# Hybrid decoder block: the gate's low-rank product in plain f32 over four column groups, x rejoined by GpSimd

## The chip, the cores and the metric

The kernel runs on one core of a Trainium2 chip. The metric is the device time of one execution in microseconds. Three runs of the kernel before gave 302.15, 302.29 and 302.38; the median is 302.29. One further execution was profiled, and the rows below come from it.

## The reference

One decoder block on 256 tokens of width 1024, all in float32. The part that matters here is the gate of the gated linear attention (GLA): its logits go through a product of rank 16.

```python
h = rms_norm(x, norm1_gain[l])
proj = h @ w_in[l]
gq, gk, gv, gr, g_low, mq, mk, mv = parts          # g_low is 16 columns of proj
gate_logit = (g_low @ w_gate_up[l] + b_gate[l]).astype(jnp.float32)
log_a = jax.nn.log_sigmoid(gate_logit) / GLA_GATE_TAU
o_gla = gla_chunked(gq, gk, gv, log_a)             # then norm, times silu(gr)
q_m, k_m = rotary(mq, positions), rotary(mk, positions)
o_moba = moba_attention(q_m, k_m, mv)              # causal softmax attention here, then norm
x = x + jnp.concatenate([o_gla, o_moba], axis=-1) @ w_out[l]
h = rms_norm(x, norm2_gain[l])
x = x + (silu(h @ w_ffn_gate[l]) * (h @ w_ffn_up[l])) @ w_ffn_down[l]
return rms_norm(x, final_norm_gain)
```

## The kernel before

**Products in halves.** Each large product splits both operands into a rounded half (hi, type fp32r) and the rest (lo) and takes three matmuls: hi·hi, hi·lo, lo·hi. Weights arrive in `raw` (three slots, 512 columns by 4 chunks, or the like, of 2048 elements a unit). ScalarE (ACT) casts a unit to `w_hi` (L877), VectorE (DVE) subtracts to get `w_lo` (L1137), and counts `lo_ready`; both rings have six slots. Units are numbered: 0 to 11 are six blocks of 512 columns of w_in (q and k of the GLA, q, k, v of the attention, v and r of the GLA), 12 to 15 w_out, then three to a phase of the feed-forward part. TensorE (PE) takes them in order and waits for `hi_ready` and `lo_ready` at the head of each (`unit_ready`).

**The start.** Tokens are transposed on TensorE into PSUM (`aux`), in eight chunks of 128 features. ACT scales each by the norm's gain into `aT_hi` (L900) and DVE makes `aT_lo` (L1141), so that the chunk x is held as two halves. Units 0 and 1 are worked on chunk by chunk: `first_row(k)` takes six matmuls for chunk k (L562, L565, L568), with the weights' halves made just ahead by ACT (L906) and DVE (L1158). DVE's queue alternates: L1141 of a chunk, L1158 of the same chunk. The semaphores are `xT_lo_ready` and `first_lo_ready`.

**The gate's product.** After the eight chunks `gate_low` computes g_low transposed, 16 values by 256 tokens. Its weights, `low_raw` (128 x 8 chunks x 16), are split by ACT (L916) and GpSimd (POOL, L477) into `low_w`, where a chunk's 128 columns hold the hi and lo halves of the 16 columns in turn, four times over. Two matmuls a chunk, with `aT_hi` and `aT_lo` as the moving side, 16 in all, accumulate all four combinations in 128 rows of a bank (L589, L590). DVE copies them to `lowT` (L1199). `logits` multiplies by `w_up`, whose rows repeat w_gate_up for hi and for lo and are zero elsewhere, so the sum over rows adds the parts (L620, plain f32). Then ACT and DVE make the log of the gate, and so on.

**Order.** Every engine's program is written out by hand; nothing is scheduled by a planner. After `gate_low` come `other_gains` (L577) and unit 2. DVE, after its last L1158, starts on the angles of the rotary embedding (L1184 to L1192), then splits unit 2 (L1137), then more of the angles, then `lowT`. The rest of its queue up to the second rotation (`rotate(1)`, L1235 to L1240) is filled in the same way; TensorE transposes the rotated keys in unit 7 (`moba_k_transposed`, L613). GpSimd builds constants until about 5 us, then does L477, then the norm's factor (L472, L473: `wide_rstd`) for each half of the tokens. `reuse_a` to `reuse_f` are buffers that hold one thing after another: `reuse_a` takes the first block's result (L894), `reuse_b` the gate's logarithms.

Of the kernel before, what the change touches and what calls it, by code (L numbers as in the profile page):

```python
# [22 lines left out]
P = 128  # L23
SEQ, D = 256, 1024
T = SEQ // P
KC = D // P
# [5 lines left out]
RANK = 16  # L32
# [12 lines left out]
RAW, RING = 3, 6  # L45
# [4 lines left out]
LOOPED = (PHASES - 3) // 2  # L50
LOW_COPIES = [P, KC, P // (2 * RANK), RANK]
SCALE = float(DV) ** -0.5
GATE_UP_BANKS = ((0, 3), (2, 1))
SQUARE = 32
QUADS = P // SQUARE
# [37 lines left out]
def build_block(nc, x, positions, norm1_gain, w_in, w_gate_up, b_gate, gla_out_gain, moba_out_gain,  # L93
                w_out, norm2_gain, w_ffn_gate, w_ffn_up, w_ffn_down, final_norm_gain, inv_freq, out):
    f32, f32r, i32 = mybir.dt.float32, mybir.dt.float32r, mybir.dt.int32
    ALU = mybir.AluOpType
# [3 lines left out]
    with ExitStack() as ctx:  # L100
# [3 lines left out]
        def sem(name):  # L104
            return ctx.enter_context(nc.semaphore(name))
# [56 lines left out]

        low_w = w_hi[:, RING - 1, 0:KC * P].rearrange("p (k r w n) -> p k r w n", k=KC, w=2, n=RANK)
        turns_hi = w_lo[:, RING - 2, 0:P]
# [76 lines left out]
        first_lo_ready = sem("first_lo_ready")  # L241
        low_hi_ready = sem("low_hi_ready")
        low_lo_ready = sem("low_lo_ready")
        low_in_psum = sem("low_in_psum")
# [85 lines left out]
        def _(sp):  # L330
# [45 lines left out]
            sp.wait_ge(up_zeroed, 1)  # L376
            for n in range(2):
                sp.dma_start(w_up[n * RANK:(n + 1) * RANK, :], w_gate_up[0]).then_inc(up_loaded, 16)
            sp.dma_start(gate_bias, b_gate.to_broadcast([P, QK])).then_inc(bias_loaded, 16)
# [51 lines left out]
        def _(pool):  # L431
# [38 lines left out]
            def wide_rstd(norm, t):  # L470
# [4 lines left out]

            pool.wait_ge(low_hi_ready, 1)
            nc.gpsimd.tensor_tensor(low_w[:, :, :, 1, :], low_raw[:, :, :].unsqueeze(2).to_broadcast(LOW_COPIES),  # L477
                                    low_w[:, :, :, 0, :].bitcast(f32), ALU.subtract).then_inc(low_lo_ready, 1)
            for t in range(T):
# [24 lines left out]
        def _(pe):  # L504
# [75 lines left out]
            def gate_low():  # L580


                pe.wait_ge(low_hi_ready, 1)
                pe.wait_ge(low_lo_ready, 1)
                pe.wait_ge(xT_hi_ready, KC)
                pe.wait_ge(xT_lo_ready, KC)
                for k in range(KC):
                    left = w_hi[:, RING - 1, k * P:(k + 1) * P]
                    nc.tensor.matmul(aux[:, 2, 0:SEQ], left, aT_hi[:, k, :], start=k == 0, stop=False)  # L589
                    last = nc.tensor.matmul(aux[:, 2, 0:SEQ], left, aT_lo[:, k, :], start=False, stop=k == KC - 1)  # L590
                last.then_inc(low_in_psum, 1)
# [24 lines left out]
            def logits():  # L616
                pe.wait_ge(lowT_ready, 1)
                pe.wait_ge(up_loaded, 32)
                for t in range(T):
                    last = nc.tensor.matmul(aux[:, 1, t * QK:(t + 1) * QK], lowT[:, t * P:(t + 1) * P], w_up[:, :], start=True, stop=True)  # L620
                last.then_inc(logits_in_psum, 1)
# [234 lines left out]
        def _(act):  # L856
# [22 lines left out]
            def split(u):  # L879
                split_as(u, fill(u), u - RING + 1 if u >= RING else None)  # L880
# [30 lines left out]
            for n in range(1, KC):  # L911
                split_first(n)
                if n % 2:
                    take_xT((n + 1, n + 2) if n < KC - 1 else ())
            act.wait_ge(low_loaded, 16)
            nc.scalar.copy(low_w[:, :, :, 0, :], low_raw[:, :, :].unsqueeze(2).to_broadcast(LOW_COPIES)).then_inc(low_hi_ready, 1)  # L916
            split(2)
            for t in range(T):
                sum_squares(0, t)
            split(3)  # L920
            take_block(0, gqk)
            split(4)
# [3 lines left out]
            nc.scalar.activation(soft, soft, ACT.Ln, bias=one[:, :]).then_inc(soft_ready, 1)  # L926
            act.wait_ge(low_in_psum, 1)
            split(5)
# [592 lines left out]
```

## Time and profile before

| | |
|---|---|
| median of 3 runs | 302.29 us |
| the profiled execution | 301.75 us |
| its span on the profile | 300.0 us |
| TensorE busy | 292.4 us (97%) |
| VectorE busy | 242.4 us (81%) |
| ScalarE busy | 171.6 us |
| GpSimd busy | 19.1 us |

The span runs from the first to the last instruction; 1.75 us of the execution lie around it. Busy times are of instructions that run, not of waits. PE is a matmul, PEld the weight load ahead of it. A plain f32 matmul appears as two records. The chain of work that ended last is followed back from the end; a merged row gives its start, its length and, after x, how many instructions it merges. A row of a timeline may give in brackets how long the engine was idle before it and what ended that.

### The profile page before, as it was taken

To read this page: it belongs to the slowest core of one execution; us is meant where nothing else is said; L and a number is where in the kernel's file an instruction comes from. 1 tells how busy PE (TensorE), PEld (TensorE's weight loads), DVE (VectorE), ACT (ScalarE), POOL (GpSimd) and SP (SyncE) were. 2 spreads that over 40 slices of the span, in tenths; PEclk is the share of its full clock that TensorE was granted. 3 is DMA by queue.
4 is the path that set the end of the run, shared out by engine and by line. 5 is a ranking of instruction groups with operands and counts; after the bars stand their busy time and mean duration, and the time that the engine had idled before them with its cause. 6 is when DMAs were issued, how large, how long until landed. Compare 5 with 4: busy or idle time off the path is not lost.

```text
span 300.0 us, 4026 instructions
## 1 busy us (share of the span) xinstructions
PE 292.4 (97%) x1373; PEld 243.3 (81%) x1373; DVE 242.4 (81%) x403; ACT 171.6 (57%) x242; POOL 19.1 (6%) x41
## 2 busy tenths in 40 slices
PE   7999999999999999999999999999999999999992
PEld 7788888788898888887888888888888888888881
DVE  1999999977879687988888888889897978787155
ACT  2898999969765897717170808080808080813123
POOL 5050100000021001300000000000000000000011
PEclk9999999999999999999999999999999999999998
DMA  7987836737867121392929292929291929030003
GB/s 235 364 289 266 263 119 251 218 131 264 298 190 227 53 92 70 95 329 90 331 82 336 79 343 69 346 66 352 63 363 47 367 54 366 25 120 0 0 0 140
DMA packets 37318, 55.45 MB, mean 185 GB/s; under 512 B 2950, under 2 KB 26554, under 8 KB 37306
## 3 DMA queue, kind: packets, MB, share of 16 engines
q1 hardware_dynamic: 37140, 55.13, 54.4%
q10 hardware_dynamic: 166, 0.17, 0.2%
q8 instruction: 7, 0.11, 0.2%
q14 instruction: 5, 0.04, 0.0%
HBM read 53.72 MB, written 1.57 MB: 184 GB/s over the span
## 4 chain that ended last, share of the span: by engine, by line
PE 94%; DMA 2%; DVE 1%; issue 1%; POOL 1%; ACT 0%; SPq 0%; POOLq 0%; DVEq 0%
PE acc L508 15%; PE acc L510 15%; PE acc L509 15%; PE aux L508 13%; PE aux L509 13%; PE aux L510 13%; DMA raw<-in_w_in 2%; PE aux L613 1%; PE acc L562 1%; PE acc L565 1%; PE acc L568 1%; PE aux L683 1%; DVE x_sb L1366 1%; PE aux L707 1%; PE aux L665 1%
## 5 line engine op out<-in xcount | busy, mean ns | idle before, releaser
L1137 DVE TENSOR_TENSOR w_lo<-raw,w_hi 128x2048 fp32r<-128x2048 f32 x47 | 105.6, 2286 | 14.5 <-ACT w_hi L877 14.4
L877 ACT CAST w_hi<-raw 128x2048 fp32r<-128x2048 f32 x47 | 87.9, 1908 | 4.4 <-DMA raw<-in_w_ffn_up 2.1
L508 PE MATMUL aux<-w_hi,aT_hi 128*128 128x512 f32 (+1 forms) x180 | 69.8, 388 | 0.0
L509 PE MATMUL aux<-w_lo,aT_hi 128*128 128x512 f32 (+1 forms) x180 | 69.7, 387 | 0.0
L510 PE MATMUL aux<-w_hi,aT_lo 128*128 128x512 f32 (+1 forms) x180 | 69.7, 387 | 0.0
L1432 DVE STREAM_TRANSPOSE reuse_c<-reuse_c 32x128 f32<-32x128 f32 x160 | 48.4, 303 | 2.4
L1080 ACT CAST pT_hi<-reuse_c 128x512 fp32r<-128x512 f32 x10 | 6.2, 621 | 72.9 <-DVE reuse_c L1432 72.9
L508 PE MATMUL acc<-w_hi,aT_hi 128*128 128x512 f32 x118 | 47.1, 399 | 0.0
L510 PE MATMUL acc<-w_hi,aT_lo 128*128 128x512 f32 x118 | 46.1, 390 | 0.0
L509 PE MATMUL acc<-w_lo,aT_hi 128*128 128x512 f32 x118 | 46.0, 390 | 0.0
L508 PEld LDWEIGHTS aux<-w_hi,aT_hi 128*128 128x128 f32 x180 | 33.8, 188 | 6.9
L510 PEld LDWEIGHTS aux<-w_hi,aT_lo 128*128 128x128 f32 x180 | 33.8, 188 | 6.9
L509 PEld LDWEIGHTS aux<-w_lo,aT_hi 128*128 128x128 f32 x180 | 33.8, 188 | 6.8
L508 PE MATMUL acc<-w_hi,pT_hi 128*128 128x512 f32 x80 | 31.3, 392 | 0.0
L510 PE MATMUL acc<-w_hi,pT_lo 128*128 128x512 f32 x80 | 31.2, 390 | 0.0
L509 PE MATMUL acc<-w_lo,pT_hi 128*128 128x512 f32 x80 | 31.2, 389 | 0.0
L510 PEld LDWEIGHTS acc<-w_hi,aT_lo 128*128 128x128 f32 x118 | 22.2, 188 | 4.8
L508 PEld LDWEIGHTS acc<-w_hi,aT_hi 128*128 128x128 f32 x118 | 22.2, 188 | 4.7 <-issue 0.2
L509 PEld LDWEIGHTS acc<-w_lo,aT_hi 128*128 128x128 f32 x118 | 22.2, 188 | 4.4
L1063 ACT ACTIVATE reuse_c<-aux,rstd 128x256 f32<-128x256 f32 x22 | 10.0, 471 | 19.1 <-PE aux L510 17.9
L508 PEld LDWEIGHTS acc<-w_hi,pT_hi 128*128 128x128 f32 x80 | 15.0, 188 | 3.4 <-issue 0.3
L510 PEld LDWEIGHTS acc<-w_hi,pT_lo 128*128 128x128 f32 x80 | 15.0, 188 | 3.2
(203 smaller groups left out, 285.0 us busy)
## 6 DMA issues: line engine op xcount, KB each, us to landing
raw<-in_w_ffn_gate SPq DMA_DIRECT2D x22, 512.0 KB, 4.3
raw<-in_w_ffn_up SPq DMA_DIRECT2D x22, 512.0 KB, 5.4
raw<-in_w_ffn_down SPq DMA_DIRECT2D x22, 512.0 KB, 6.0
raw<-in_w_in SPq DMA_DIRECT2D x20, 512.0 KB, 4.8
raw<-in_w_out SPq DMA_DIRECT2D x8, 512.0 KB, 4.3
raw<-in_w_in SPq DMA_DIRECT2D x8, 256.0 KB, 6.2
x_sb<-in_x SPq DMA_DIRECT2D x2, 512.0 KB, 3.7
m_moves<-reuse_c SPq DMA_DIRECT2D x1, 512.0 KB, 2.7
```

What stands on the lines that cost most here:

```text
L508: nc.tensor.matmul(dst, left_hi[:, k, tok], right_hi, start=first, stop=False)
L509: nc.tensor.matmul(dst, left_hi[:, k, tok], right_lo, start=False, stop=False)
L510: return nc.tensor.matmul(dst, left_lo[:, k, tok], right_hi, start=False, stop=last)
L562: nc.tensor.matmul(acc[:, t, :], aT_hi[:, k, toks[t]], right_hi, start=k == 0, stop=False)
L565: nc.tensor.matmul(acc[:, t, :], aT_hi[:, k, toks[t]], right_lo, start=False, stop=False)
L568: last = nc.tensor.matmul(acc[:, t, :], aT_lo[:, k, toks[t]], right_hi, start=False, stop=k == KC - 1)
L613: last = nc.tensor.transpose(aux[:, bank, n * P:(n + 1) * P], src, ident[:, :])
L877: nc.scalar.copy(w_hi[:, slot % RING, :], raw[:, slot % RAW, :]).then_inc(hi_ready, 1)
L1063: nc.scalar.activation(silu_g[:, t, :], aux[:, GATE_UP_BANKS[parity][t], 0:FF], ACT.Silu, scale=rstd[:, 1, t:t + 1]).then_inc(silu_ready, 1)
L1080: nc.scalar.copy(dst, src.rearrange("p (k s) -> p k s", k=2)).then_inc(hiddenT_hi_ready, 1)
L1137: nc.vector.tensor_tensor(w_lo[:, slot % RING, :], raw[:, slot % RAW, :], w_hi[:, slot % RING, :].bitcast(f32), ALU.subtract).then_inc(lo_ ...
L1432: last = nc.vector.transpose(cols[SQUARE * c:SQUARE * (c + 1), :, :, g, :], rows[SQUARE * g:SQUARE * (g + 1), :, :, c, :])
```

## The change

Nothing is split for the gate's product any more. GpSimd adds `aT_hi` and `aT_lo` back together, two chunks at a time, into four tiles `xT_raw` of 128 x 512 (in `reuse_a` and `reuse_b`), and copies `low_raw` twice side by side into a `low_w` of 8 x 32 columns (in `reuse_d`). `gate_low` is eight plain f32 matmuls with 32 columns each. Chunk k writes the rows of group k mod 4, so that chunks 0 to 3 start the four groups and 4 to 7 complete them. `w_up` repeats w_gate_up at the head of each group of 32 rows, so its load is four DMAs on SP's queue where it was two. ACT's L916 is gone, and ACT waits for `low_in_psum` before it writes `reuse_a`, not later.

```diff
@@ TensorE
             def gate_low():
-                pe.wait_ge(low_hi_ready, 1)
-                pe.wait_ge(low_lo_ready, 1)
-                pe.wait_ge(xT_hi_ready, KC)
-                pe.wait_ge(xT_lo_ready, KC)
+                pe.wait_ge(low_w_ready, 1)
+                pe.wait_ge(xT_raw_ready, KC // 2)
                 for k in range(KC):
-                    left = w_hi[:, RING - 1, k * P:(k + 1) * P]
-                    nc.tensor.matmul(aux[:, 2, 0:SEQ], left, aT_hi[:, k, :], start=k == 0, stop=False)
-                    last = nc.tensor.matmul(aux[:, 2, 0:SEQ], left, aT_lo[:, k, :], start=False, stop=k == KC - 1)
+                    group = slice(k % QUADS * SQUARE, (k % QUADS + 1) * SQUARE)
+                    last = nc.tensor.matmul(aux[group, 2, 0:SEQ], low_w[:, k, :, :].rearrange("p w n -> p (w n)"),
+                                            xT_raw[k // 2][:, k % 2 * SEQ:(k % 2 + 1) * SEQ], start=k < QUADS, stop=k >= QUADS)
                 last.then_inc(low_in_psum, 1)
@@ GpSimd
-            pool.wait_ge(low_hi_ready, 1)
-            nc.gpsimd.tensor_tensor(low_w[:, :, :, 1, :], low_raw[:, :, :].unsqueeze(2).to_broadcast(LOW_COPIES),
-                                    low_w[:, :, :, 0, :].bitcast(f32), ALU.subtract).then_inc(low_lo_ready, 1)
+            def rejoin_xT(pair):
+                pool.wait_ge(xT_lo_ready, 2 * pair + 2)
+                hi, lo = (v[:, 2 * pair:2 * pair + 2, :].rearrange("p k s -> p (k s)").bitcast(f32) for v in (aT_hi, aT_lo))
+                nc.gpsimd.tensor_tensor(xT_raw[pair], hi, lo, ALU.add).then_inc(xT_raw_ready, 1)
+
+            for pair in range(2):
+                rejoin_xT(pair)
+            pool.wait_ge(low_loaded, 16)
+            nc.gpsimd.tensor_copy(low_w, low_raw[:, :, :].unsqueeze(2).to_broadcast(LOW_COPIES)).then_inc(low_w_ready, 1)
+            for pair in range(2, KC // 2):
+                rejoin_xT(pair)
@@ ACT
-            act.wait_ge(low_loaded, 16)
-            nc.scalar.copy(low_w[:, :, :, 0, :], low_raw[:, :, :].unsqueeze(2).to_broadcast(LOW_COPIES)).then_inc(low_hi_ready, 1)
             split(2)
             for t in range(T):
                 sum_squares(0, t)
             split(3)
+            act.wait_ge(low_in_psum, 1)
             take_block(0, gqk)
...
-            act.wait_ge(low_in_psum, 1)
             split(5)
@@ SP
-            for n in range(2):
-                sp.dma_start(w_up[n * RANK:(n + 1) * RANK, :], w_gate_up[0]).then_inc(up_loaded, 16)
+            for n in range(QUADS):
+                sp.dma_start(w_up[n * SQUARE:n * SQUARE + RANK, :], w_gate_up[0]).then_inc(up_loaded, 16)
```

GpSimd's queue in before, from the last of its constants (L466) to the norm's factor of the first tokens (L472, L473):

```order
L466 AFFINE_SELECT tri_mid<-tri_mid 64x64 [waits pool_seq]
L477 TENSOR_TENSOR w_hi<-low_raw,w_hi 128x32x16 [waits low_hi_ready,consts_built]
L472 TENSOR_SCALAR ms<-ss 128x1 [waits ss_ready]
L473 TENSOR_TENSOR rstd<-ms,minus_half 128x1 [waits pool_seq]
L472 TENSOR_SCALAR ms<-ss 128x1 [waits ss_ready]
```

The same place now, where L480 is `rejoin_xT` and L485 the copy of `low_raw`:

```order
L467 AFFINE_SELECT tri_mid<-tri_mid 64x64 [waits pool_seq]
L480 TENSOR_TENSOR reuse_a<-aT_hi,aT_lo 128x512 [waits xT_lo_ready,consts_built]
L480 TENSOR_TENSOR reuse_a<-aT_hi,aT_lo 128x512 [waits xT_lo_ready]
L485 COPY reuse_d<-low_raw 128x256 [waits low_loaded]
L480 TENSOR_TENSOR reuse_b<-aT_hi,aT_lo 128x512 [waits xT_lo_ready] x2
L473 TENSOR_SCALAR ms<-ss 128x1 [waits ss_ready]
```

One operation became five, and all but the copy follow DVE's `xT_lo_ready`.

TensorE's queue in before, from the last matmul of the first rows to unit 2, of the 16 matmuls of `gate_low` the first two:

```order
L568 MATMUL acc<-w_hi,aT_lo 128x512
L589 MATMUL aux<-aT_hi,w_hi 128x256 [waits xT_hi_ready,xT_lo_ready,low_lo_ready,low_hi_ready]
L590 MATMUL aux<-aT_lo,w_hi 128x256
...
L577 MATMUL aux<-ident,reuse_d 128x10 [waits rows_loaded,gains_ready]
L508 MATMUL acc<-w_hi,aT_hi 128x512 [waits lo_ready,hi_ready]
```

The same place now:

```order
L577 MATMUL acc<-w_hi,aT_lo 128x512
L596 MATMUL aux<-reuse_a,reuse_d 32x256 [waits xT_raw_ready,low_w_ready]
L596 MATMUL aux<-reuse_a,reuse_d 32x256 x3
L596 MATMUL aux<-reuse_b,reuse_d 32x256 x4
L586 MATMUL aux<-ident,reuse_d 128x10 [waits rows_loaded,gains_ready]
L517 MATMUL acc<-w_hi,aT_hi 128x512 [waits lo_ready,hi_ready]
```

The product waits for GpSimd's last addition and its copy; what follows it is unchanged. DVE's queue has the same instructions in the same order.

## Rows read from the trace of the kernel before

**Rows 1.** The page's busy times, and TensorE's granted clock in 40 slices.
```profile
PE 292.4 (97%) x1373; PEld 243.3 (81%) x1373; DVE 242.4 (81%) x403; ACT 171.6 (57%) x242; POOL 19.1 (6%) x41
...
PEclk9999999999999999999999999999999999999998
```
**Rows 2.** The page's chain that ended last, by engine.
```profile
PE 94%; DMA 2%; DVE 1%; issue 1%; POOL 1%; ACT 0%; SPq 0%; POOLq 0%; DVEq 0%
```
**Rows 3.** The chain, 18 to 26 us: start, length, what.
```profile
19.02 0.12 PE aux L589
...
20.93 0.15 PE aux L577
21.09 0.43 PE acc L508
...
24.04 0.86 PE aux L620 x4
```
**Rows 4.** DVE's timeline, 8 to 45 us: start, length, instruction.
```profile
8.93 0.68 DVE L1158 TENSOR_TENSOR w_lo<-raw,w_hi 128x512 fp32r<-128x512 f32 x1
...
9.92 0.68 DVE L1158 TENSOR_TENSOR w_lo<-raw,w_hi 128x512 fp32r<-128x512 f32 x1
...
14.49 0.48 DVE L1141 SCALAR_TENSOR_TENSOR aT_lo<-aux,gains,aT_hi 128x256 fp32r<-128x256 f32 x1
14.89 1.54 DVE L1158 TENSOR_TENSOR w_lo<-raw,w_hi 128x512 fp32r<-128x512 f32 x1
...
17.11 0.23 DVE L1177 TENSOR_SCALAR reuse_e<-reuse_e 128x128 f32<-128x128 f32 x1
...
18.22 2.29 DVE L1137 TENSOR_TENSOR w_lo<-raw,w_hi 128x2048 fp32r<-128x2048 f32 x1
...
22.79 2.29 DVE L1137 TENSOR_TENSOR w_lo<-raw,w_hi 128x2048 fp32r<-128x2048 f32 x1
```
**Rows 5.** DVE's timeline further on, to the second rotation's end.
```profile
35.76 0.69 DVE L1245 SCALAR_TENSOR_TENSOR reuse_c<-reuse_a,reuse_c 128x512 f32<-128x512 f32 x1 [0.32 <-ACT reuse_c L934]
...
52.22 0.69 DVE L1240 TENSOR_TENSOR reuse_e<-reuse_e,mv 128x512 f32<-128x512 f32 x1
```
**Rows 6.** TensorE's timeline where the rotated keys are transposed.
```profile
52.70 0.39 PE L510 MATMUL acc<-w_hi,aT_lo 128*128 128x512 f32 x1
52.97 1.09 PE L613 MATMUL aux<-ident,reuse_e 128*128 128x128 f32 x8
```
**Rows 7.** The chain, 74 to 81 us: products without and with column groups.
```profile
75.76 2.68 PE aux L683 x24
78.44 0.59 PE aux L695 x8
79.03 0.43 PE acc L508
```
**Rows 8.** POOL's timeline, 8 to 45 us.
```profile
14.59 1.29 POOL L477 TENSOR_TENSOR w_hi<-low_raw,w_hi 128x512 fp32r<-128x512 f32 x1 [9.48 <-ACT w_hi L916]
18.56 2.00 POOL L472 TENSOR_SCALAR ms<-ss 128x1 f32<-128x1 f32 x1 [2.68 <-ACT reuse_f L883]
...
21.30 0.19 POOL L472 TENSOR_SCALAR ms<-ss 128x1 f32<-128x1 f32 x1
```
**Rows 9.** The instructions and the DMA that touch the tile low_raw.
```profile
L369 SPq DMA_DIRECT2D low_raw<-in_w_in x1: 478/478/478, 6.2 to 6.2; - x1
...
DMA to landing us min/median/max: 6.4/6.4/6.4
```
**Rows 10.** ACT's timeline, 8 to 45 us.
```profile
15.52 1.91 ACT L877 CAST w_hi<-raw 128x2048 fp32r<-128x2048 f32 x1 [1.07 <-DMA raw<-in_w_in]
...
19.42 1.90 ACT L877 CAST w_hi<-raw 128x2048 fp32r<-128x2048 f32 x1
21.30 0.69 ACT L894 ACTIVATE reuse_a<-acc,rstd 128x512 f32<-128x512 f32 x1
```
**Rows 11.** TensorE's timeline in the first rows: chunk 2's product with the weights' lo half.
```profile
11.15 0.62 PE L565 MATMUL acc<-w_lo,aT_hi 128*128 128x512 f32 x2
```

More of the change, by code:

```diff
@@ L50 @@
 LOOPED = (PHASES - 3) // 2
-LOW_COPIES = [P, KC, P // (2 * RANK), RANK]
+LOW_COPIES = [P, KC, 2, RANK]
 SCALE = float(DV) ** -0.5
@@ L161, in build_block @@
         rot_tmp = mv[:, :, 0:HEADS * HALF].rearrange("p t (h d) -> p t h d", h=HEADS)
-        low_w = w_hi[:, RING - 1, 0:KC * P].rearrange("p (k r w n) -> p k r w n", k=KC, w=2, n=RANK)
+        low_w = reuse_d[:, 512:512 + KC * SQUARE].rearrange("p (k w n) -> p k w n", k=KC, n=RANK)
+        xT_raw = [half[:, :].rearrange("p (b n) -> p b n", b=2)[:, b, :] for half in (reuse_a, reuse_b) for b in range(2)]
         turns_hi = w_lo[:, RING - 2, 0:P]
@@ L241, in build_block @@
         first_lo_ready = sem("first_lo_ready")
-        low_hi_ready = sem("low_hi_ready")
-        low_lo_ready = sem("low_lo_ready")
+        low_w_ready = sem("low_w_ready")
+        xT_raw_ready = sem("xT_raw_ready")
         low_in_psum = sem("low_in_psum")
@@ L617, in logits @@
                 pe.wait_ge(lowT_ready, 1)
-                pe.wait_ge(up_loaded, 32)
+                pe.wait_ge(up_loaded, 16 * QUADS)
                 for t in range(T):
```

## The prediction

> **What bounds the kernel now.** I read the page's busy shares first: TensorE is busy 292.4 of 300.0 us and its clock is granted in full from the second slice on [rows 1]. The chain that ended last gives it 94% [rows 2]. From 7.64 us on it never starves, so any microsecond it stands still, or does less, is the kernel's, unless another engine is late just behind. So the second question, asked of the timelines, is how late the others run around the change. The gate's low-rank product takes 19.02 to 20.93 on the chain, 1.91 us for 16 matmuls at 0.12 [rows 3]. The next unit waits for VectorE's half-subtraction of unit 2 (L1137), which ends at 18.22 + 2.29 = 20.51 [rows 4]; TensorE gets there at 21.09. That is half a microsecond of slack, and no wait. VectorE itself then runs without a gap but one of 0.32 us until 52.91, where the second rotation's last instruction ends [rows 5]. The transposes that need it start at 52.97, 0.27 after the matmul before instead of 0.23 [rows 6]: no slack at all. VectorE's queue from 8 to 53 us is a second critical path beside TensorE's, and what counts is which moves more.
>
> **What the product saves.** Sixteen matmuls go. Eight in plain f32 come, in two rounds of four column groups. A plain f32 instruction with 256 moving columns is two records: L620 shows 4 records for 2 instructions in 0.86 us, 0.215 each [rows 3]. Eight instructions are 16 records: 3.44 us if they follow one another, 0.86 if four groups run side by side. Nothing here uses groups of 32, but L695 uses two of 64: 8 records in 0.59 us (0.074 each) where L683, the same length without groups, takes 2.68 for 24 (0.112), and the matmul after L695 takes 0.43 on the chain instead of 0.23 [rows 7]. So groups overlap, and leaving them costs 0.2. I take 0.86 + two changes of 0.2 = 1.3 us; ends 0.86 and 3.44. Taken alone that is a gain of 0.6. It can't be had alone.
>
> The page "TensorE: Matmul & The Clock Gate" of the Trainium skill, section "Part 3: Packing small matmuls — row/col tiling", gives 2.38 times for three column groups; by that rate four would take about 1.1 us here (an estimate). Rows 7 agree in direction only. Nothing of the sum hangs on it.
>
> **What GpSimd's additions cost.** This is the term that decides. In before, GpSimd does one two-input operation of 512 elements, L477, from 14.59 for 1.29 us, to 15.88 [rows 8]. VectorE's L1158 issued at 14.89 took 1.54 us instead of 0.68 and ended at 16.43, 0.55 after GpSimd [rows 4, 8]. It stood still: 0.86 lost. The other way round, L472, a one-element operation of 0.19 us, took 2.00 and ended at 20.56, just behind L1137's 20.51 [rows 4, 8]. So, where VectorE's instruction reads two operands in SBUF and GpSimd's reads SBUF too, one keeps the other out for its whole length. L1141, whose source is in PSUM, kept its 0.48 at 14.49 with GpSimd starting in it [rows 4].
>
> The Trainium skill has this as a rule against the change: "SBUF — State Buffer", section "Who interferes with whom", says that a VectorE instruction with two SBUF inputs contends with a GpSimd one that reads SBUF, and that the first to start holds the port for its whole length. The trace agrees, by the 0.86 us and the 2.00 us above.
>
> The change puts four additions of 128x512 there, and a copy of 128x256, and takes L477 away. Each addition waits for a second half of x (L1141). Behind that L1141 VectorE at once issues a subtraction L1158, so the addition is queued behind it. Let the subtraction end at E. GpSimd's start-up of about 0.14 is then hidden (0.05 instead of 0.19 past L1137's end), so the addition ends at E + 1.15. The next subtraction would have ended at E + 0.99 (9.61, then 10.60 [rows 4]); now it ends 0.55 behind the addition, at E + 1.70. Delay: 0.71. In between stands one L1141, which releases nothing new for GpSimd, since additions wait for pairs. So:
> - additions 1, 2, 3 (from about 9.6, 12.3, 15.0) each hold one subtraction: 3 x 0.71 = 2.13;
> - addition 4 (from about 17.7 to 18.8) meets the small operations: L1177 starts 0.68 after the last subtraction and would end at 0.91 [rows 4]. One source in SBUF, a form no row shows beside GpSimd: 0 to 0.35, and I take 0.35 as L472 also waited with one source;
> - the copy: 256 elements, between 0.19 and half of L477's 1.29, in the gap beside an L1141 of 0.40: 0 to 0.25, I take 0.05. low_raw is asked for at 6.2 and lands 6.4 us later, 12.6 [rows 9], in time for it;
> - L477's 0.86 goes.
>
> Sum for the end of L1137 on unit 2: 2.13 + 0.35 + 0.05 - 0.86 = +1.67, so 22.2 instead of 20.51. ACT loses its copy of low_raw, but behind it ACT waits for a load until 15.52 [rows 10], so nothing comes of it.
>
> **What TensorE sees.** In the first rows a chunk costs it six matmuls of 0.23, 1.37 us, against VectorE's 0.99, so its cover grows. At chunk 2 it is thin: first needed at 11.15 [rows 11], delivered before at 10.60, now at 11.31: a stall of 0.2. Chunks 4 and 6 (delays 1.42 and 2.13 against a cover of 1.3 and 2.0 plus that 0.2) just hold or cost another 0.1. The product starts at 19.2 to 19.3; x is rejoined at about 18.8. It ends near 20.6. Then TensorE stands until 22.2: unit 2 begins 1.67 - 0.5 = 1.17 later than before. Everything the product saves falls into this hole, and so would anything up to 2.8 us. Two more loads of w_up are issued on SP, each at about the 0.48 us of low_raw's issue [rows 9]; they push the load of unit 3 by up to 1.0. ACT read that unit at 19.42 [rows 10] and VectorE only at 22.79 [rows 4], so three microseconds cover it. ACT's wait for low_in_psum now stands before L894, at 21.30 in before [rows 10], with the product done by then.
>
> **To the end.** VectorE is 1.67 late, TensorE 1.17. VectorE's only gap, 0.32 before L1245 [rows 5], gives back 0.32 (it waits there for ACT and through it for TensorE, which is less late). So the second rotation is done 1.35 later, and TensorE, without slack there, follows: +1.35. After 53 us VectorE has waits of its own for TensorE and nothing of the change is left. The profiled execution took 301.75: 303.1. The median of the runs is 302.29, 0.54 above it: **303.6**.
>
> **Rivals.**
> - *The additions are cheap* (faster). Their operands are plain rows, while L477 read a broadcast and a view with gaps. With VectorE's 0.68 for the same size as the low end, an addition would hold a subtraction 0.1, in all 0.3 - 0.86 = -0.56 for unit 2, at 19.95. Then TensorE's own 1.3 instead of 1.91 decides: -0.6, 301.7; with a quicker product -0.9, 301.4. No row of GpSimd speaks for it.
> - *The two cancel*. With additions of 0.95 us: 3 x 0.37 + 0.03 + 0.05 - 0.86 = +0.33, less the gap of 0.32: no change, 302.3.
> - *The groups don't overlap* (slower for another reason). 3.44 from 19.25 is 22.7, with L577 22.85; unit 2 begins 22.85 - 21.09 = 1.8 later, over VectorE's 1.35: 304.1. It decides from a product longer than 2.8 us. Rows 7 speak against it.
> - Upwards of the forecast: start-up not hidden, 3 x 0.14, and 0.2 for the copy: 304.2.
>
> **How the numbers follow.** Forecast 0.60, groups one by one 0.12, cancelling 0.15, cheap additions 0.13. A measurement tells about 0.2%, 0.6 us, from no change. Faster than 301.7: 0.12. Within: 0.16 (the cancelling case and the edges of the others). Slower: 0.72. The forecast's own spread is 302.9 to 304.2; the range runs from the edge of the cheap case, 301.9, to the serial one with a dearer addition, 304.7.
>
> **What would show it.** Right: four additions of about 1.3 us on GpSimd; every second subtraction L1158 of the first rows at 1.2 to 1.4 us instead of 0.68; L1137 on unit 2 ending at about 22.2; TensorE idle for 1 to 2 us before unit 2 with VectorE as releaser, and a little at the transposes near 54. The product itself shorter than 1.91 us. Wrong: subtractions at 0.68 beside additions, or a TensorE that runs from the product into unit 2 without a wait.

## The result, and the profile after

| | before | after |
|---|---|---|
| median beside each other | 302.31 us (6 runs, 301.86 to 302.86) | 304.65 us (6 runs, 304.12 to 305.27) |
| the profiled execution | 301.75 us, span 300.0 | 304.88 us, span 302.9 |

After takes 1.0083 times as long, with an interval of 1.0073 to 1.0094. Against the 302.29 of the forecast's base that is 304.8, outside the range's upper end of 304.7 by a little; the median as measured, 304.65, is just inside. The kernel is slower, as forecast, and by more.

TensorE's busy time is *up* by 1.5 us although its work became less, and one slice of its clock is no longer full, where [rows 1] has all nines until the end:

```profile
PE 293.9 (97%) x1373; PEld 243.6 (80%) x1373; DVE 244.2 (81%) x403; ACT 170.8 (56%) x241; POOL 25.6 (8%) x45
...
PEclk9997999999999999999999999999999999999997
```

GpSimd's timeline in after, where [rows 8] has one operation ahead of L472:

```profile
9.15 1.61 POOL L480 TENSOR_TENSOR reuse_a<-aT_hi,aT_lo 128x512 f32<-128x512 f32 x1 [4.04 <-DVE aT_lo L1146]
11.79 1.69 POOL L480 TENSOR_TENSOR reuse_a<-aT_hi,aT_lo 128x512 f32<-128x512 f32 x1 [1.03 <-DVE aT_lo L1146]
13.43 0.86 POOL L485 COPY reuse_d<-low_raw 128x256 f32<-128x256 f32 x1
14.51 1.69 POOL L480 TENSOR_TENSOR reuse_b<-aT_hi,aT_lo 128x512 f32<-128x512 f32 x1 [0.22 <-DVE aT_lo L1146]
17.23 1.70 POOL L480 TENSOR_TENSOR reuse_b<-aT_hi,aT_lo 128x512 f32<-128x512 f32 x1 [1.03 <-DVE aT_lo L1146]
```

VectorE's in after, to be held against [rows 4, 5]. L1163 is the subtraction of the first rows (L1158 before), L1142 a whole unit's (L1137), L1250 is L1245:

```profile
8.91 0.68 DVE L1163 TENSOR_TENSOR w_lo<-raw,w_hi 128x512 fp32r<-128x512 f32 x1
...
9.91 1.41 DVE L1163 TENSOR_TENSOR w_lo<-raw,w_hi 128x512 fp32r<-128x512 f32 x1
...
12.63 1.40 DVE L1163 TENSOR_TENSOR w_lo<-raw,w_hi 128x512 fp32r<-128x512 f32 x1
...
15.35 1.41 DVE L1163 TENSOR_TENSOR w_lo<-raw,w_hi 128x512 fp32r<-128x512 f32 x1
...
18.44 0.57 DVE L1182 TENSOR_SCALAR reuse_e<-reuse_e 128x128 f32<-128x128 f32 x1
...
19.91 2.29 DVE L1142 TENSOR_TENSOR w_lo<-raw,w_hi 128x2048 fp32r<-128x2048 f32 x1
...
27.83 0.88 DVE L1214 SCALAR_TENSOR_TENSOR reuse_b<-aux,rstd,mv 128x256 f32<-128x256 f32 x2 [1.06 <-PE aux L627]
...
38.59 0.69 DVE L1250 SCALAR_TENSOR_TENSOR reuse_c<-reuse_a,reuse_c 128x512 f32<-128x512 f32 x1 [0.27 <-ACT reuse_c L939]
```

Three subtractions wait for an addition and take 1.4 instead of 0.68, the first small operation takes 0.57 instead of 0.23, and unit 2's half is done at 22.20 instead of 20.51: 1.69 later. VectorE was level before that (8.91 against 8.93 in [rows 4]). TensorE's timeline in after, against [rows 3, 6]:

```profile
19.35 0.64 PE L596 MATMUL aux<-reuse_a,reuse_d 128*32 128x256 f32 x8
19.81 0.61 PE L596 MATMUL aux<-reuse_b,reuse_d 128*32 128x256 f32 x8
20.35 0.23 PE L586 MATMUL aux<-ident,reuse_d 10*128 10x10 f32 x1
22.35 0.47 PE L517 MATMUL acc<-w_hi,aT_hi 128*128 128x512 f32 x1 [1.77 <-DVE w_lo L1142]
...
24.28 0.63 PE L517 MATMUL acc<-w_hi,aT_hi 128*128 128x512 f32 x1
24.71 0.63 PE L518 MATMUL acc<-w_lo,aT_hi 128*128 128x512 f32 x1
...
55.81 1.09 PE L620 MATMUL aux<-ident,reuse_e 128*128 128x128 f32 x8
```

The product takes 1.0 us (19.35 to 20.35). Then TensorE stands still for 1.77. From 23.4 on its matmuls start 0.43 apart, where 0.23 is usual. The view of stretches gives the clock. Its columns: the stretch, its length, busy time of PE, PEld, DVE, ACT and POOL, then the granted clock, the DMA share and GB/s:

```profile
20.40:22.30 1.90, 0.18 (x5) 0.08 (x1) 1.90 (x2) 1.64 (x2) 1.85 (x1) 1.00 0.91 353
...
23.20:26.50 3.30, 3.30 (x10) 2.55 (x9) 3.20 (x6) 2.25 (x2) 0.00 (x0) 0.51 0.96 302
```

The clock was granted at 0.51, its lower level of 1.2 GHz, for 3.3 us behind the stop. The logits' matmuls came late, VectorE waited 1.06 us for them (its row at 27.83), and the rotated keys are transposed at 55.81, 2.84 after before's 52.97. The span is longer by 2.9.

### The profile page after: what moved, and what is told of

It is laid out like the page before. It is cut to its first block, busy times and chain, and to the rows that moved or that the text cites. A ratio compares the mean times of both kernels' runs of the same rounds, so it can differ in the third digit from the quotient of the medians.

```text
span 302.9 us, 4029 instructions
## 1 busy us (share of the span) xinstructions
PE 293.9 (97%) x1373; PEld 243.6 (80%) x1373; DVE 244.2 (81%) x403; ACT 170.8 (56%) x241; POOL 25.6 (8%) x45
## 4 chain that ended last, share of the span: by engine, by line
PE 91%; DVE 6%; issue 1%; ACT 1%; POOL 1%; POOLq 0%; DVEq 0%; ACTq 0%
PE acc L517 15%; PE acc L518 15%; PE acc L519 15%; PE aux L518 13%; PE aux L519 13%; PE aux L517 13%; DVE w_lo L1163 2%; PE aux L620 1%; PE acc L534 1%; DVE aT_lo L1146 1%; PE aux L690 1%; DVE w_lo L1142 1%; DVE x_sb L1371 1%; PE aux L543 1%; PE aux L714 1%
## 5 line engine op out<-in xcount | busy, mean ns | idle before, releaser
L1142 DVE TENSOR_TENSOR w_lo<-raw,w_hi 128x2048 fp32r<-128x2048 f32 x47 | 105.6, 2286 | 15.0 <-ACT w_hi L884 14.9
L518 PE MATMUL acc<-w_lo,aT_hi 128*128 128x512 f32 x118 | 46.7, 396 | 0.0
L1068 ACT ACTIVATE reuse_c<-aux,rstd 128x256 f32<-128x256 f32 x22 | 9.9, 470 | 19.3 <-PE aux L519 18.0
```

The source lines that it names most:

```text
L518: nc.tensor.matmul(dst, left_hi[:, k, tok], right_lo, start=False, stop=False)
L1068: nc.scalar.activation(silu_g[:, t, :], aux[:, GATE_UP_BANKS[parity][t], 0:FF], ACT.Silu, scale=rstd[:, 1, t:t + 1]).then_inc(silu_ready, 1)
L1142: nc.vector.tensor_tensor(w_lo[:, slot % RING, :], raw[:, slot % RAW, :], w_hi[:, slot % RING, :].bitcast(f32), ALU.subtract).then_inc(lo_ ...
```

## The experiments

Each was timed in five rounds beside before. Ratios are to the before timed with it, with their 95% intervals in brackets.

**Is the clock's fall a cost of its own? (e1)** The changed kernel, and 14 idle-work matmuls where TensorE stood still:

```diff
             other_gains()
+            warm_up(14)
```

> Kernel after with 14 matmuls of 256 columns that do no work, put between L586 and unit 2, into the 1.77 us in which TensorE stood still. Theory 1 (GpSimd's additions make VectorE late, TensorE stands still for 1.8 us, and this standing still is what lowers its clock to 1.2 GHz for the 3.3 us that follow): unit 2 still begins at about 22.4 behind L1142, the granted clock stays at full, the 12 matmuls after it take 0.23 instead of 0.43, and 1.5 us come back: 303.6 to 303.8 where after is 304.7. Rival (the clock falls because of the eight 32-column matmuls themselves, or at random): the clock is still at half after unit 2's start, and the time stays at 304.5 to 304.8.

Measured: 304.16, ratio 1.0069 (1.0054 to 1.0084), clock 0.997 in the profile. TensorE's timeline:

```profile
20.68 1.93 PE L534 MATMUL acc<-w_lo 128*128 128x256 f32 x14
22.54 0.47 PE L517 MATMUL acc<-w_hi,aT_hi 128*128 128x512 f32 x1
22.84 0.39 PE L518 MATMUL acc<-w_lo,aT_hi 128*128 128x512 f32 x1
...
54.85 1.09 PE L620 MATMUL aux<-ident,reuse_e 128*128 128x128 f32 x8 [0.27 <-DVE reuse_e L1246]
```

and VectorE's:

```profile
20.09 2.29 DVE L1143 TENSOR_TENSOR w_lo<-raw,w_hi 128x2048 fp32r<-128x2048 f32 x1
...
37.63 0.69 DVE L1251 SCALAR_TENSOR_TENSOR reuse_c<-reuse_a,reuse_c 128x512 f32<-128x512 f32 x1 [0.43 <-ACT reuse_c L940]
```

No fall, matmuls 0.23 apart, and the transposes about a microsecond earlier than in after. But the level was missed upward by 0.4 to 0.6: VectorE's gap before L1251 is 0.43, not closed. So the forecast's "gives back 0.32" is in doubt. The medians alone don't price the fall: this ratio, 1.0069, lies between after's 1.0083 and the 1.0063 of after's second set (e0, next). The price comes from the profiles below.

**How often does the clock fall? (e0)** The changed kernel again.

> The changed kernel once more, on the chip of the next three, to see how often TensorE's clock falls in it. If standing still 1.77 us before unit 2 lowers the clock in some executions and not in others, the executions split into spans of about 302.1 (clock 0.994 or higher) and 302.6 to 303.3 (clock 0.988 or 0.989), median 304.3 to 304.9. If the fall in the first profile was an accident, nearly all executions are at 304.1 to 304.3.

Measured: 303.70 (303.41 to 305.01), ratio 1.0063 (1.0045 to 1.0081). Five of six executions have a mean clock of 0.994 or more and 303.4 to 304.3 us; one has 0.990 and 305.01. The profiled one, after a stop of 1.75 us, kept its clock. With the first six: seven executions with 0.994 or more, 303.4 to 304.3, middle 303.9; five with 0.988 to 0.990, 304.6 to 305.3, middle 304.9. The second lot costs 1.0 more; that is rough, as it is 0.7 within the first set and 1.5 within this one. The executions do split, as expected, but the upper lot is the smaller one here, so that the median lies under the 304.3 to 304.9 of the expectation. That the slower ones have the fall is seen in one profile and inferred for the rest. A low mean clock alone proves little: one execution of e13 below has 0.945 and takes an ordinary 302.28.

**Do the groups run side by side? (e2)** All eight chunks in the first group of 32 columns, with w_up loaded once (start and stop follow; not shown):

```diff
-                    group = slice(k % QUADS * SQUARE, (k % QUADS + 1) * SQUARE)
+                    group = slice(0, SQUARE)
```

> Kernel after with all eight chunks in one column group (rows 0 to 31), accumulating one after another, and w_up loaded once. If the four groups run side by side in after, the 16 records now take 16 x 0.215 = 3.4 us instead of 1.0, from about 19.3 to 22.8. Theory 1: the longer product fills the hole, unit 2 begins at about 23.0 (0.6 later than in after), but the clock stays at full: about 303.9 to 304.3, that is faster than after although the product is 2.4 us longer. Rival (the 32-column matmuls lower the clock): 305.3 or more. Rival (groups give nothing): product 1.0 us as in after, and 304.7.

Measured: 304.23, ratio 1.0073 (1.0060 to 1.0086). TensorE's timeline:

```profile
19.36 1.91 PE L596 MATMUL aux<-reuse_a,reuse_d 128*32 128x256 f32 x8
21.11 1.89 PE L596 MATMUL aux<-reuse_b,reuse_d 128*32 128x256 f32 x8
22.93 0.23 PE L586 MATMUL aux<-ident,reuse_d 10*128 10x10 f32 x1
23.08 0.50 PE L517 MATMUL acc<-w_hi,aT_hi 128*128 128x512 f32 x1
```

The product takes 3.57 us instead of 1.0, so the groups do overlap, and yet the kernel isn't slower than after: the product fills the hole, and TensorE never stops. It overfills it a little, as VectorE's timeline shows:

```profile
27.04 0.88 DVE L1214 SCALAR_TENSOR_TENSOR reuse_b<-aux,rstd,mv 128x256 f32<-128x256 f32 x2 [0.29 <-PE aux L627]
```

VectorE waits 0.29 for the logits, and from the end of unit 2's half (22.18) to L1250 (37.82) it takes 15.64 instead of the 15.25 that e8 below finds at full clock. So of the 2.6 us that the groups save about 0.4 would arrive, and none when the clock falls behind the stop that they leave.

**Is it GpSimd's reads that cost? (e3)** The additions become writes of the same tiles, with x left out of the gate's product:

```diff
-                nc.gpsimd.tensor_tensor(xT_raw[pair], hi, lo, ALU.add).then_inc(xT_raw_ready, 1)
+                nc.gpsimd.memset(xT_raw[pair], 0.0).then_inc(xT_raw_ready, 1)
```

> Kernel after with GpSimd's four additions replaced by four memsets of the same tiles behind the same waits: GpSimd then writes only and reads nothing. Left out: x in the gate's product, which multiplies zeros. Theory 1 (what holds VectorE is a GpSimd operation that reads SBUF beside a subtraction that reads two operands there): all subtractions L1163 at 0.68 us, L1142 of unit 2 ends at 19.7 instead of 22.2, no hole, no fall of the clock, unit 2 begins at about 20.5 behind the shorter product: 301.7 to 301.9, about 0.5 below before. Rival (any GpSimd operation, or the waits themselves, make VectorE late): subtractions still at 1.2 us or more where a memset runs, unit 2 at 21 or later, 302.3 or more.

Measured: 301.64, ratio 0.9984 (0.9975 to 0.9993). VectorE's timeline, the same subtraction that took 1.41:

```profile
10.05 0.68 DVE L1162 TENSOR_TENSOR w_lo<-raw,w_hi 128x512 fp32r<-128x512 f32 x1
...
17.53 2.29 DVE L1141 TENSOR_TENSOR w_lo<-raw,w_hi 128x2048 fp32r<-128x2048 f32 x1
```

All are 0.68, unit 2's half ends at 19.82, and TensorE takes it at 20.24 with no stop. Making x costs 2.4 to 3.0 us (ratios of 1.0063 and 1.0083 against 0.9984, the clock's fall included). The half microsecond under before isn't the product's alone. TensorE's timeline:

```profile
52.27 1.09 PE L619 MATMUL aux<-ident,reuse_e 128*128 128x128 f32 x8
```

The transposes start 0.70 earlier than before's 52.97. TensorE was free for them 0.79 earlier (52.14 for 52.93), by its shorter product; VectorE's rotation was done 0.69 earlier (52.22 for 52.91), because L477, which stopped it for 0.86, is gone. Both were level in before, and the later one decides. No run takes one of the two away alone.

**Do the additions alone cost the whole? (e7)** Before with its old product, and only the four additions put in, their result unused (ACT waits for them before it writes `reuse_a`; not shown):

```diff
+            for pair in range(3):
+                rejoin_xT(pair)
             pool.wait_ge(low_hi_ready, 1)
             nc.gpsimd.tensor_tensor(low_w..., ALU.subtract).then_inc(low_lo_ready, 1)
+            rejoin_xT(3)
```

> Kernel before with nothing but the four additions added to GpSimd's queue (L477 between the third and the fourth), their result unused; the product is the old one, 16 matmuls. Theory 1: four GpSimd operations hold a subtraction by 0.71 each, the last additon meets the small operations (0.35), L477's old 0.86 goes: L1137 of unit 2 ends 2.3 later, at 22.9; the old product ends at about 21.2, so TensorE stands still for 1.8 us, and the clock falls: 302.3 + 2.0 + 1.5 = 305.8; if the clock holds, 304.3. Rival (the loss is in the new product or its waits, not in the additions): 302.3.

Measured: 304.55, ratio 1.0083 (1.0069 to 1.0096), as after. GpSimd's timeline:

```profile
16.44 1.76 POOL L486 TENSOR_TENSOR w_hi<-low_raw,w_hi 128x512 fp32r<-128x512 f32 x1
18.15 1.76 POOL L481 TENSOR_TENSOR reuse_b<-aT_hi,aT_lo 128x512 f32<-128x512 f32 x1
```

and TensorE's:

```profile
23.34 0.47 PE L518 MATMUL acc<-w_hi,aT_hi 128*128 128x512 f32 x1 [1.28 <-DVE w_lo L1148]
...
55.65 1.09 PE L623 MATMUL aux<-ident,reuse_e 128*128 128x128 f32 x8 [0.28 <-DVE reuse_e L1251]
```

Five operations of 512 elements now hold VectorE, whose half of unit 2 ends at 23.19. TensorE stood still for 1.28 us, and the clock held. That the time equals after's is chance: here VectorE is 2.68 late at full clock, there 1.69 with most executions at the lower clock.

**How much of a delay of VectorE arrives? (e8)** Before, with three quarters of unit 2's subtraction done twice:

```diff
+            then(nc.vector.tensor_tensor(w_lo[:, 2, 0:1536], raw[:, 2, 0:1536], w_hi[:, 2, 0:1536].bitcast(f32), ALU.subtract))
             split(2)
```

> The kernel before with one thing added: VectorE does 1536 of unit 2's 2048 columns of the half-subtraction once more, ahead of the whole, about 1.75 us, and nothing else changes. It tells how much of a delay of VectorE there arrives at the end. Theory 1 (VectorE's gap of 0.32 us before L1245 hangs on ACT's chain, which starts from VectorE's own logits, so it moves along and gives nothing back): plus 1.75, 304.0, with the second rotation's transposes idle for about 0.3 and no fall of the clock (TensorE idle for 1.2 before unit 2). The prediction's step (the gap gives 0.32 back): plus 1.4, 303.6. With a fall of the clock 305 or more.

Measured: 304.11, ratio 1.0069 (1.0056 to 1.0082): at least 1.7 us, which is theory 1; the prediction's plus 1.4 would be 1.0046. VectorE's timeline:

```profile
18.43 1.76 DVE L1194 TENSOR_TENSOR w_lo<-raw,w_hi 128x1536 fp32r<-128x1536 f32 x1
20.23 2.29 DVE L1137 TENSOR_TENSOR w_lo<-raw,w_hi 128x2048 fp32r<-128x2048 f32 x1
...
37.76 0.69 DVE L1247 SCALAR_TENSOR_TENSOR reuse_c<-reuse_a,reuse_c 128x512 f32<-128x512 f32 x1 [0.43 <-ACT reuse_c L934]
```

The gap is still there (0.43). Two distances tell it best: from the end of unit 2's half to the start of L1245, and from there to the transposes. Before: 20.51, 35.76, 52.97, so 15.25 and 17.21. Here: 22.52, 37.76, 54.97, so 15.24 and 17.21. In e1: 22.38, 37.63, 54.85, so 15.25 and 17.22. In these profiles not a hundredth is given back. In e7 the two together are 32.46, as before. After has 16.39 for the first. The changed kernel's other profile (e0), with the same stop and a full clock, has 15.25, so 1.14 is the price of the fallen clock:

```profile
20.45 2.29 DVE L1142 TENSOR_TENSOR w_lo<-raw,w_hi 128x2048 fp32r<-128x2048 f32 x1
...
37.99 0.69 DVE L1250 SCALAR_TENSOR_TENSOR reuse_c<-reuse_a,reuse_c 128x512 f32<-128x512 f32 x1 [0.44 <-ACT reuse_c L939]
```

Why the gap moves along is seen on ACT in before. Its work up to L934 starts behind VectorE's own logits (L1209):

```profile
25.90 0.63 ACT L924 ACTIVATE reuse_b<-reuse_b 128x512 f32<-128x512 f32 x1 [0.78 <-DVE reuse_b L1209]
```

**Does the stop alone lower the clock? (e10)** The same with the whole subtraction repeated, 2.29 us, so that TensorE stands still about as long as in after, behind the old product.

> The same with all 2048 columns repeated, about 2.34 us: TensorE stands still for about 1.76 us before unit 2, as long as in the changed kernel, but after the old product. If it is the standing still that lowers the clock, some or most executions show a granted clock of about 0.5 for some 3 us from 23 on: plus 2.34 and about 0.5 to 1.2 more, 305.0 to 305.7. If it is something else in the changed kernel (the plain f32 products in groups of 32 columns), the clock holds: 304.6 (304.3 by the prediction's step).

Measured: 305.34 (304.27 to 306.07), ratio 1.0108 (1.0088 to 1.0128). Three executions at 0.989 (305.7 to 306.1), three at 0.995 or more (304.3 to 304.9). In the profiled one TensorE stopped for 1.68 us; the stretch behind it:

```profile
23.20:26.50 3.30, 3.30 (x9) 2.64 (x10) 3.10 (x8) 2.48 (x2) 0.21 (x1) 0.58 0.73 210
```

VectorE's distance from unit 2's half (22.99) to L1245 (39.40) is 16.41 here, so the fall costs 1.16. It belongs to the stop, not to the new product, and at this length it comes in some executions and not in others.

**Can x be had without GpSimd? (e5, e11, e12, e14)** ACT multiplies the transposes in PSUM by the gain once more, into `xT_raw`; GpSimd adds nothing. e5:

```diff
+            take_raw(range(4))          # nc.scalar.mul(xT_raw..., aux..., gains...), 128x256 each
             split(2)
-            for t in range(T):
-                sum_squares(0, t)
+            take_raw(range(4, KC))
+            sum_squares(0, 0)
             split(3)
+            sum_squares(0, 1)
@@ SP
-            sp.dma_start(low_raw..., 16 columns of w_in)
+            for w in range(2):
+                sp.dma_start(low_w[:, :, w, :], the same 16 columns)
```

> The product over four column groups stays, but ACT writes the raw x itself from the transposes in PSUM (eight multiplications of 128x256 by the gain, about 0.42 us each, 3.3 us in all), low_w comes by two DMAs, and GpSimd does nothing for the product. Theory 1 (the loss was GpSimd's hold on VectorE's subtractions): all subtractions are 0.68, VectorE's half of unit 2 ends at about 19.8, unit 2 starts at about 20.3 without a wait, which is 0.7 earlier than before. ACT has 2.4 us of idle time between 13.8 and 35.7 for 3.3 us of added work, less its own copy of low_raw of 0.65, so its chain to the gate's cumulative sum is late by up to 0.2: 302.2 to 302.5. Rival (ACT's chain has no part in it): the whole 0.6 to 0.7 arrives, 301.5 to 301.7. Rival (the x written by anyone costs as much): 303.5 or more.

Measured: 306.09, ratio 1.0133 (1.0117 to 1.0149): far above theory 1 and the first rival. The second rival's "303.5 or more" is met, but e11 will show another cause. ACT's timeline:

```profile
16.45 1.91 ACT L874 CAST w_hi<-raw 128x2048 fp32r<-128x2048 f32 x1 [1.32 <-DMA raw<-in_w_in]
...
22.55 1.91 ACT L874 CAST w_hi<-raw 128x2048 fp32r<-128x2048 f32 x1 [1.69 <-DMA raw<-in_w_in]
```

Units 2 and 3, which ACT read at 15.52 and 19.42 in [rows 10], are waited for. VectorE's subtractions were 0.68 each, as meant, but its half of unit 2 began behind a wait of 1.41 for ACT. Issuing the two loads of 16 columns held SP's queue for 2.64 us (0.58 for the one in e11), so the loads of units 2 and 3 were issued from 8.57 on instead of 6.38. e11 takes the second load of 16 columns away again:

```diff
-            for w in range(2):
-                sp.dma_start(low_w[:, :, w, :], ...)
+            sp.dma_start(low_w[:, :, 0, :], ...)     # GpSimd zeroes low_w[:, :, 1, :] at the start
```

> As e5 (ACT writes the raw x), but low_w comes by one DMA into its first 16 columns of each chunk, and GpSimd zeroes the second 16 at the start, when it is free. If what made e5 slow was its second load of 16 columns (the loads of units 2 and 3 landed 0.9 and 3 us later than before, and ACT waited 1.3 and 1.7 us for them with its raw chunks and sums queued behind), those waits go. Theory: subtractions of 0.68, unit 2 from about 20.3 (21.0 before), ACT's chain to the cumulative sum between 0.3 earlier and 0.2 later than before: 301.6 to 302.3. Rival (ACT has no room for 3.1 us more, wherever the loads are): 303.5 or more.

Measured: 303.18, ratio 1.0041 (1.0028 to 1.0055), 2.9 us less than e5. That one load of 64 KB in short rows was dear, and it is all that differs but for GpSimd's zeroing. What is left, 1.1 us over before, falls between theory and rival. GpSimd's timeline in e11:

```profile
22.67 1.59 POOL L474 TENSOR_SCALAR ms<-ss 128x1 f32<-128x1 f32 x1 [1.75 <-ACT reuse_f L881]
```

and VectorE's:

```profile
21.92 2.29 DVE L1141 TENSOR_TENSOR w_lo<-raw,w_hi 128x2048 fp32r<-128x2048 f32 x1
25.00 0.88 DVE L1213 SCALAR_TENSOR_TENSOR reuse_b<-aux,rstd,mv 128x256 f32<-128x256 f32 x2 [0.79 <-POOL rstd L475]
```

The second sum of squares came later, so GpSimd's one-element operation fell into VectorE's half of unit 3, was shut out until 24.2, and the logits waited for it. That wait only used up what had been gained: VectorE's logits begin at 25.00, exactly where before's do. What is lost is on ACT:

```profile
24.99 0.69 ACT L892 ACTIVATE reuse_a<-acc,rstd 128x512 f32<-128x512 f32 x1 [1.83 <-POOL rstd L475]
...
27.37 0.63 ACT L929 ACTIVATE reuse_b<-reuse_b 128x512 f32<-128x512 f32 x1
```

ACT waits 1.83 for the same rstd with its cast of unit 4 queued behind, and so starts on the logits at 27.37 instead of 25.90. These 1.47 are what the end of the chain shows: L1249 at 37.22 instead of 35.76, the transposes at 54.43 instead of 52.97. e12 puts both sums behind ACT's cast of unit 3, e14 ahead of it, with work of VectorE moved into its wait:

```diff
@@ e12, against e11
             take_raw(range(4, KC))
-            sum_squares(0, 0)
             split(3)
+            sum_squares(0, 0)
             sum_squares(0, 1)
@@ e14, against e11: ACT, then VectorE
             sum_squares(0, 0)
-            split(3)
             sum_squares(0, 1)
+            split(3)
...
+            for part in two_pi_parts(5)[3:]:      # stood behind the logits
+                take_off(turns_hi.bitcast(f32), part)
+                take_off(turns_lo, part)
             split(3)
```

> The same, with ACT's cast of unit 3 ahead of both sums of squares, so that VectorE's half of unit 3 does not wait for it. If ACT's order is what is left of the cost in e11, this is faster by 0.2 to 0.6; if rstd (which the gate's logits need, and which now comes later) decides, slower by up to 0.5.

> e11 with the sums of squares both ahead of ACT's cast of unit 3, as the kernel before has them, and with VectorE's four operations on the angles that stood after the logits moved ahead of its half of unit 3, to fill its wait for ACT. In e11 the logits waited for GpSimd's second rstd (idle 0.79 on VectorE, 1.83 on ACT), which took 2.5 us because GpSimd's small operation was shut out by VectorE's half of unit 3. If that is what kept e11 0.4% above before, this one has rstd by 22, the logits at 24.6 to 25.0 as before, and ends level with before or 0.2 under it: 301.9 to 302.3. If ACT's added work as such is the cost (it has 2.4 us of idle time for 2.5), it stays at 302.7 or more.

Measured: e12 304.48, ratio 1.0077 (1.0063 to 1.0092), worse than e11 by 1.3, over twice what the rival gave: VectorE waits 1.71 for rstd. e14 302.62, ratio 1.0022 (1.0013 to 1.0032), better than e11 by 0.6 but not level, between theory and rival. rstd was in time there. But VectorE's four moved operations took 1.3 us (22.40 to 23.70) where it would have waited about 0.8 for ACT's cast (an estimate: the cast ends at 23.08), so the logits began at 25.91 and ACT's chain behind them at 26.82, for 25.90 before. Its transposes started at 53.89, 0.92 late by just this, behind 1.28 us of idle TensorE: the time that the product had saved, and more, was waited away there.

**Half of the change without its costs (e13).** ACT writes chunks 0 to 3 in its idle time; they go in plain f32, one to a group, and chunks 4 to 7 stay in halves, in group 0 (the weights' views are shortened):

```diff
+                for k in range(QUADS):
+                    nc.tensor.matmul(aux[k * SQUARE:(k + 1) * SQUARE, 2, 0:SEQ], low_f[:, k], reuse_a[:, k * SEQ:(k + 1) * SEQ], start=True, stop=k > 0)
+                for k in range(QUADS, KC):
+                    nc.tensor.matmul(aux[0:SQUARE, 2, 0:SEQ], low_w[:, k - QUADS], aT_hi[:, k, :], start=False, stop=False)
+                    nc.tensor.matmul(aux[0:SQUARE, 2, 0:SEQ], low_w[:, k - QUADS], aT_lo[:, k, :], start=False, stop=k == KC - 1)
```

> The kernel before with half of the change, and neither of its costs. Chunks 0 to 3 of the gate's product are plain f32, one in each of the four column groups, from a raw x that ACT writes in its idle stretch at 13.8 us (four of 128x256, 1.6 us); chunks 4 to 7 stay in halves, 32 columns wide, in group 0. GpSimd's two operations shrink to 128x64 each, so they hold VectorE for at most 0.3 instead of 0.86; w_up comes by one DMA. Theory: VectorE's half of unit 2 ends 0.5 to 0.8 earlier than before (19.7 to 20.0), the product takes about 0.5 + 8 x 0.12 = 1.5 instead of 1.91, so unit 2 starts 0.4 earlier and the end comes 0.3 to 0.5 earlier: 301.6 to 301.9, against 302.1. Rival (a plain f32 product in four groups pays 0.4 for going in and out, with half the chunks in it nothing is left): 302.0 to 302.3.

Measured: 301.98, ratio 0.9996 (0.9987 to 1.0006): level with before. TensorE's timeline:

```profile
19.64 0.64 PE L593 MATMUL aux<-reuse_a,reuse_d 128*32 128x256 f32 x8
20.21 0.31 PE L597 MATMUL aux<-aT_hi,w_hi 128*32 128x256 f32 x1
...
21.41 0.50 PE L511 MATMUL acc<-w_hi,aT_hi 128*128 128x512 f32 x1
```

Product and gains take 1.77 us where before's took 2.16 by the same view (18.86 to 21.02). But unit 2 starts at 21.41, 0.39 later than in before, although VectorE's half of it was ready at 20.18: in this execution TensorE began its first rows at 8.49, for 7.64 in before, as its first transposes took 1.91 us instead of 1.04. The logits came late by it, VectorE waited 0.55 for them, and the transposes start at 53.33. After, e0 and e1 show the same slow first transposes, before and e3 don't, so it doesn't follow the change; what causes it is open. The profile therefore can't show what half of the change is worth, and the interval allows a gain of up to 0.4. Theory and rival are not told apart. No version here that computes the whole block beats before.

## Why the prediction was right in its mechanism and short in its size

Two steps failed. VectorE's gap was to give back 0.32 and gave back nothing. And the clock behind TensorE's stop was put at nothing, without a reason, where its fall costs 1.14. The rest of the sum held.

- **The additions decide** (right). Forecast 2.13 for three subtractions; they took 1.41, 1.40 and 1.41, three times 0.73 more. Forecast 0.35 for the small operation, measured 0.34. Sum +1.67, measured 1.69. e3 and e7 show it from both sides: reads taken away, the cost goes; additions alone, it is there. An addition ended about 1.17 behind the subtraction ahead of it, for 1.15 forecast. "SBUF — State Buffer" of the Trainium skill, section "Who interferes with whom", says the contention is with a GpSimd instruction that reads SBUF, not with one that only writes it; e3's 0.68 beside writes of the same size agrees.
- **The copy of low_raw** (right). It took 0.86 and stalled no subtraction by itself.
- **The product** (right in kind). 1.0 us, for 1.3 forecast. The forecast's 0.2 for leaving the groups was read from the 0.43 behind L695; [rows 3] has the same 0.43 behind L577, which uses no such groups. All of the saving falls into the hole, as said. "Anything up to 2.8 us" would, too, was a little too much: e2's 3.57 cost VectorE 0.4. It started at 19.35, for 19.2 to 19.3 forecast, partly by luck: TensorE had begun the first rows 0.44 later than before's (8.08 for 7.64), and the stalls forecast in them came to about 0.1 at chunk 2.
- **TensorE's wait before unit 2** (right). It idled 1.77 us, in the forecast's 1 to 2, released by VectorE.
- **"gives back 0.32"** (wrong). The prediction took VectorE's gap before L1245 for a wait on something that is not late. It hangs on ACT's exponentials (L934), and these end a queue that starts from VectorE's own logits: Abs, Exp, a table load, Ln, a cast, a table load, a cast, three exponentials, with no idle time in it. What is late on VectorE makes ACT late by the same. e8, e1 and e7 show 32.46 us from unit 2's half to the transposes, as before. With this term out, the forecast would be 303.9, and that is the middle of the seven executions in which the mean clock was high. The exact fit is partly luck: against their own befores these lie 1.8 (two, first set) and 1.5 (five, e0) above, on either side of the forecast's 1.67.
- **The clock** (left out, and the larger miss). The prediction read in [rows 1] that the clock was full and TensorE hardly idle, and then had TensorE stop for 1 to 2 us without asking what the clock would do. After the stops of 1.77, 1.75 and 1.68 us it fell in two profiles of three, after 1.28 (e7) and 1.22 (e8) it held, and a fall costs 1.14 and 1.16 us by the distances in after and e10, about 1.0 by the two lots of executions. That puts the medians at 303.7 to 304.65, according to how many executions have it.

The first median, 304.65, is 1.05 over the forecast: 0.3 for the gap, and the remaining 0.75 is put down to the clock, as four of its six executions had the lower mean. The profiled execution is 3.13 over before's: 1.69 for the additions and 1.14 for the clock are seen in it; the last 0.3 lies in small terms and outside the span (2.9 longer).

## What to carry to other kernels

Before a gap of an engine is counted as slack against a delay of that same engine, follow its releaser back: if the releaser's queue starts from the delayed engine's own result, the gap moves with the delay and gives nothing. Where a sum makes TensorE stop for as long as here, 1.7 us, in a kernel that never stopped before, put the lower clock behind the stop as a term of its own, with a chance. Where two engines' queues arrive level, as at the transposes here, work taken off one of them arrives only as far as the other comes earlier too. And work handed to an engine that looks idle (GpSimd here, ACT in e5 to e14) is priced by what it locks or what queues behind it, not by its own length: four additions of 1.2 us each held VectorE for 2.5 (1.7 net of L477), to save 0.9 of a product.

## What the runs showed of the hardware that was not expected

- Sixteen records of a plain f32 product, 32 columns wide, took 1.0 us over four column groups and 3.57 in one (e2): 3.6 times.
- Behind a stop of 1.77 us (after) the granted clock was 0.51 for 3.3 us, behind one of 1.75 in the same kernel (e0) it stayed at 1.0. It fell behind 1.68 (e10) and 2.13 us (e5, at 33), and held behind 1.47 and 1.53 (e12) and 1.51 (e11).
- GpSimd's writes of 128x512 took 0.53 us each and held nothing (e3); its additions of that size took about 1.17.
- With a second load of 128 x 8 pieces of 64 bytes SP's issuing of the pair took 2.64 us instead of 0.58, and ACT got to unit 3 at 22.55 instead of 19.63 (e5 against e11).
